# Three slots instead of two for the dilated attention, with its first jobs inside the gate block

## The reference

```
s = einsum(q, k) * DIL_SCALE           # per block: 128 queries, at most 2 x 128 keys
s = where(band & has_prev, s, -inf)
m = s.max(-1);  e = exp(s - m);  l = e.sum(-1);  acc = einsum(e, v)
...                                    # for each of the three groups, then
w = exp(m - m.max(groups));  o_b = sum(w * acc) / sum(w * l)
y_b = (o_b * silu(gb)) @ w_pb
```

## Time and profile before

| | |
|---|---|
| time, median of 3 runs | 1364.68 us (1364.15 to 1368.87) |
| profiled execution, its own time | 1366.24 us |
| its span | 1364.4 us, 22980 instructions |
| PE busy | 1218.7 us (89%) |
| DVE busy | 698.7 us (51%) |
| ACT busy | 509.3 us (37%) |
| POOL busy | 255.6 us (19%) |
| mean granted TensorE clock | 0.919 |

### The profile page before, as it was taken

One profiled execution on the slowest core, in us unless ns is written; L12 is line 12 of the kernel. 1 busy time (PEld: TensorE's weight loads), 2 busy tenths in 40 slices (PEclk: granted clock), 3 DMA queues, 4 the chain that ended last, 5 costly groups with the idle time before them and its releaser, 6 DMA issues.

```text
span 1364.4 us, 22980 instructions
## 1 busy us (share of the span) xinstructions
PE 1218.7 (89%) x7616; PEld 998.0 (73%) x7616; DVE 698.7 (51%) x1611; ACT 509.3 (37%) x1187; POOL 255.6 (19%) x262
## 2 busy tenths in 40 slices
PE   5897869998898799999977999998999899997987
PEld 1276757887687577787756999998998899997431
DVE  4317977176573332120414676766676667676421
ACT  1323545143243333323313554544454445453010
POOL 0033530266874003344420000000000000000000
PEclk9998869899998559999998999999999999998578
DMA  8632010122233003332264301323132323225005
GB/s 273 186 112 70 17 41 1 28 78 74 81 90 101 8 16 94 93 85 78 88 205 140 97 14 36 88 66 88 55 85 66 85 58 84 69 72 186 0 29 158
DMA packets 79418, 112.40 MB, mean 82 GB/s; under 512 B 8628, under 2 KB 50757, under 8 KB 79294
## 3 DMA queue, kind: packets, MB, share of 16 engines
q1 hardware_dynamic: 76214, 101.59, 26.0%
q0 software_dynamic: 1440, 5.11, 1.0%
q10 hardware_dynamic: 1648, 4.23, 0.9%
HBM read 105.21 MB, written 5.68 MB: 81 GB/s over the span
## 4 chain that ended last, share of the span: by engine, by line
PE 60%; DVE 15%; issue 8%; ACT 6%; POOL 5%; DMA 5%; SPq 2%; ACTq 0%; DVEq 0%; POOLq 0%
PE ps L1417 18%; PE ps L1081 6%; PE ps L1082 6%; PE ps L1083 6%; PE ps L1398 5%; PE ps L1096 3%; DVE ssq L2184 3%; PE ps L1443 3%; DMA raw<-in_w_ada 2%; ACT cT_hi L879 2%; PE ps L1463 2%; PE ps L1226 1%; PE ps L1220 1%; PE ps L1296 1%; PE ps L1307 1%
## 5 line engine op out<-in xcount | busy, mean ns | idle before, releaser
L960 POOL TENSOR_TENSOR wlo<-raw,whi 128x512 fp32r<-128x512 f32 (+3 forms) x148 | 171.3, 1161 | 447.1 <-ACT whi L624 446.9
L1081 PE MATMUL ps<-whi,hT_hi 128*128 128x512 f32 (+3 forms) x512 | 191.4, 374 | 31.0 <-POOL wlo L960 21.2
L1417 PE MATMUL ps<-wq_hi,cT_hi 128*128 128x260 f32 x1024 | 217.8, 294 | 0.4 <-ACT sq L908 0.4
L1417 PE MATMUL ps<-wq_hi,cT_lo 128*128 128x260 f32 x1024 | 206.8, 283 | 0.0
L1417 PE MATMUL ps<-wq_lo,cT_hi 128*128 128x260 f32 x1024 | 206.4, 283 | 0.0
L2184 DVE TENSOR_REDUCE ssq<-sq 128x8 f32<-128x512 f32 x256 | 172.6, 682 | 64.6 <-ACT sq L908 62.2
L624 ACT ACTIVATE whi<-raw 128x512 fp32r<-128x512 f32 (+3 forms) x148 | 83.2, 564 | 327.4 <-PE ps L1078 255.7
L1083 PE MATMUL ps<-whi,hT_lo 128*128 128x512 f32 (+3 forms) x512 | 187.1, 365 | 0.0
L1082 PE MATMUL ps<-wlo,hT_hi 128*128 128x512 f32 (+3 forms) x512 | 186.8, 365 | 0.0
L1417 PEld LDWEIGHTS ps<-wq_hi,cT_lo 128*128 128x128 f32 x1024 | 158.6, 189 | 0.0
L1417 PEld LDWEIGHTS ps<-wq_hi,cT_hi 128*128 128x128 f32 x1024 | 157.9, 190 | 0.8 <-ACT sq L908 0.8
(11 more groups left out here) (401 smaller groups left out, 1681.5 us busy)
## 6 DMA issues: line engine op xcount, KB each, us to landing
cn<-in_cache_mla SPq DMA_DIRECT2D x256, 144.0 KB, 2.1
raw<-in_w_in SPq DMA_DIRECT2D x64, 256.0 KB, 2.7
raw<-in_w_ada SPq DMA_DIRECT2D x48, 256.0 KB, 3.1
raw<-in_w_out SPq DMA_DIRECT2D x32, 256.0 KB, 3.0
sdk<-in_cw SPq DMA_DIRECT2D x3, 1536.0 KB, 11.2
raw<-in_w_in SPq DMA_DIRECT2D x32, 128.0 KB, 2.1
raw<-in_w_pa SPq DMA_DIRECT2D x16, 256.0 KB, 2.9
x_tiles<-in_x_prompt ACTq DMA_DIRECT2D x4, 512.0 KB, 5.6
```

Of the source, the lines that this page charges most:

```text
L960: nc.gpsimd.tensor_tensor(out=wlo[:, s % NHL, 0:width], in0=raw[:, j % NRAW, 0:width], in1=whi[:, s % NHL, 0:width].bitcast(F32), op=ALU.s ...
L1081: mm(out, hi[:, k, c], bh, start=st, stop=False)
L1417: last = mm(ps[:, 3 + 2 * (u % 2) + f, 0:260], a[c], wq[:, c, f, w], start=c == 0 and a is hi and wq is wq_hi, stop=c == 1 and a is lo)
```

## The change

Three things change, all around `pair_attention`.

**Banks.** The four tiles of `GB` take two banks, two tiles side by side in each (`PLACE`), with their sample rows in bank 7; the accumulation of a bank begins only with the tile at column 0 and is closed only by the second tile (`SHARES_BANK`). The items `TE` go to the banks of the tiles of `GA` as VectorE releases them (`HELD_BY`). The freed banks make three pairs of score banks. The turned bank and the output bank become single.

**Order around the gate.** `heads_turned(2)` moves from between `GA` and `GB` to ahead of chunk 2 of `GB`, and ScalarE rounds chunks 3 and 4 of `GB` ahead of its copies of those items. Ahead of chunk 4 both `qk(0)` and `qk(1)` are issued. ScalarE and VectorE do the exponentials and masks of jobs 0 and 1 before `GB` is copied out; each copy of a gate tile waits for both tiles of its bank.

**Order in the loop.** Masks, exponentials and scores are one job further ahead: TensorE `tr(n+1)`, `qk(n+3)`, `pv(n)`; VectorE copy of an even n, then `masks_max(n+2)`, `finish(n-1)`; ScalarE copy of an odd n, then `exp(n+2)`. `tr(n+1)` waits for the copy of n, and `pv(n)` for `finish(n-1)`. `pair_probs` becomes three tiles.

```diff
@@ -137,8 +137,23 @@
 MLA_JOBS = [(i, h, i + 1) for i in range(NT) for h in range(HM)]
-_gb = [(ITEM["GB"] + t) % BANKS for t in range(BANKS)]
-PAIR_SCORES, PAIR_OUT, PAIR_TURNED = ((_gb[5], _gb[6]), (_gb[0], _gb[1])), (_gb[3], _gb[4]), (7, _gb[2])
+_ga = [(ITEM["GA"] + t) % BANKS for t in range(BANKS)]
+PAIR_SLOTS, PAIR_AHEAD = 3, 2
+PAIR_SCORES, PAIR_OUT, PAIR_TURNED = (_ga[0:2], _ga[2:4], _ga[5:7]), 7, _ga[4]
+PLACE = {ITEM["GB"] + t: (_ga[5 + t // 2], t % 2 * BW) for t in range(NT)}
+PLACE[ITEM["GBs"]] = (7, 0)
+SHARES_BANK = [ITEM["GB"], ITEM["GB"] + 2]
+HELD_BY = {ITEM["GB"] + t: ITEM["GA"] - 2 + t // 2 for t in range(NT)}
+HELD_BY[ITEM["GBs"]] = None
+for _t in range(4):
+    PLACE[ITEM["TE"] + _t], HELD_BY[ITEM["TE"] + _t] = (_ga[_t], 0), ITEM["GA"] + _t
...
+
+def place(idx):
+
+    return PLACE.get(idx, (idx % BANKS, 0))
@@ -154,7 +169,7 @@
-    return 6 + chunk % 2 if chunk < N_MLA_CHUNKS else PAIR_TURNED[(chunk - N_MLA_CHUNKS) % 2]
+    return 6 + chunk % 2 if chunk < N_MLA_CHUNKS else PAIR_TURNED
@@ -328,7 +343,9 @@
         gb_sig = v3(put("gate_b_sigmoid", [P, NT * BW], V + 16 * K1), NT, BW)
-        pair_p = v3(put("pair_probs", [P, 2 * 512], W + 18432), 2, 512)
+        assert 229344 - V >= 62 * K1 + 256, 229344 - V
+        pair_p = [put(f"pair_probs{n}", [P, 512], o)[:, :]
+                  for n, o in enumerate((W + 18432, W + 20480, V + 60 * K1 + 256))]
@@ -629,7 +646,8 @@
             def bank(idx, w, n=P, start=0):
-                return ps[start:start + n, idx % BANKS, 0:w]
+                b, c = place(idx)
+                return ps[start:start + n, b, c:c + w]
@@ -705,23 +723,24 @@
                         h = 2 * hp + hh
-                        p = pair_p[:, n % 2, 256 * hh:256 * hh + nb * P]
+                        p = pair_p[n % PAIR_SLOTS][:, 256 * hh:256 * hh + nb * P]
...
-                split_to(FIRST["GB"] + COUNT["GB"])
-                exp(0)
+                for n in range(PAIR_AHEAD):
+                    exp(n)
...
                 for t in range(NT):
+                    act.wait_ge(z_done, ITEM["GB"] + t // 2 * 2 + 2)
...
                 for n in range(len(PAIR_JOBS)):
-                    if n + 1 < len(PAIR_JOBS):
-                        exp(n + 1)
...
                         pt_copy(act, nc.scalar.activation, N_MLA_CHUNKS + n, 2 * PAIR_JOBS[n][3], pt_a, (ACT.Copy,))
+                    if n + PAIR_AHEAD < len(PAIR_JOBS):
+                        exp(n + PAIR_AHEAD)
@@ -827,7 +846,9 @@
             mix_gates("GA", AW)
+            split_to(FIRST["GB"] + 5)
             heads_in_order(2, ITEM["TE"])
+            split_to(FIRST["GB"] + COUNT["GB"])
@@ -1047,8 +1068,9 @@
-                if idx >= BANKS:
-                    wait_evac(pe, idx - BANKS)
+                held = HELD_BY.get(idx, idx - BANKS if idx >= BANKS else None)
+                if held is not None:
+                    wait_evac(pe, held)
@@ -1071,8 +1093,9 @@
                             wait_bank(idx)
-                        out = ps[:, idx % BANKS, 0:w]
-                        st, en = k == 0, k == nk - 1
+                        bank, col = place(idx)
+                        out = ps[:, bank, col:col + w]
+                        st, en = k == 0 and col == 0, k == nk - 1
@@ -1080,7 +1103,7 @@
                             mm(out, hi[:, k, c], bl, start=False, stop=False)
-                            last = mm(out, lo[:, k, c], bh, start=False, stop=en)
+                            last = mm(out, lo[:, k, c], bh, start=False, stop=en and idx not in SHARES_BANK)
@@ -1100,7 +1123,7 @@
                 for col, rows_out_, src in parts:
-                    last = nc.tensor.transpose(ps[0:rows_out_, idx % BANKS, col:col + n_in], src, ident[0:n_in, 0:n_in])
+                    last = nc.tensor.transpose(ps[0:rows_out_, place(idx)[0], col:col + n_in], src, ident[0:n_in, 0:n_in])
@@ -1277,7 +1300,6 @@
             block_of("GA", ITEM["GA"], range(5), hThi, hTlo, hTs)
-            heads_turned(2, ITEM["TE"])
@@ -1285,9 +1307,10 @@
                     near, i, hp, nb = PAIR_JOBS[n]
-                    if n >= 2:
-                        pe.wait_ge(masked, N_MLA + n - 1)
-                    banks = PAIR_SCORES[n % 2]
+                    if n >= PAIR_SLOTS:
+                        pe.wait_ge(masked, N_MLA + n - PAIR_SLOTS + 1)
+                    slot = n % PAIR_SLOTS
+                    banks = PAIR_SCORES[slot]
@@ -1300,30 +1323,34 @@
                     pe.wait_ge(exp_done, N_MLA + n + 1)
-                    if n >= 2:
-                        wait_pt(pe, c - 2)
+                    if n >= 1:
+                        wait_pt(pe, c - 1)
...
                         o = 256 * (q // nb) + P * (q % nb)
-                        last = nc.tensor.transpose(ps[:, PAIR_TURNED[n % 2], q * P:(q + 1) * P], pair_p[:, n % 2, o:o + P], ident)
+                        last = nc.tensor.transpose(ps[:, PAIR_TURNED, q * P:(q + 1) * P], pair_p[n % PAIR_SLOTS][:, o:o + P],
+                                                   ident)
...
                 def first_scores(k):
-                    if k == 5:
+                    if k == 2:
+                        heads_turned(2, ITEM["TE"])
+                    elif k == 4:
...
                         qk(0)
+                        qk(1)
...
                 tr(0)
-                wait_evac(pe, ITEM["GB"] + 1)
-                qk(1)
+                wait_evac(pe, ITEM["GB"] + NT - 1)
+                qk(2)
...
                         tr(n + 1)
-                    if n + 2 <= last_job:
-                        qk(n + 2)
-                    if n >= 2:
-                        pe.wait_ge(o_done, N_MLA + n - 1)
+                    if n + PAIR_SLOTS <= last_job:
+                        qk(n + PAIR_SLOTS)
+                    if n >= 1:
+                        pe.wait_ge(o_done, N_MLA + n)
@@ -1335,7 +1362,7 @@
                                 vcl[:, b, i, h * 64:(h + 1) * 64]
-                            last = mm(ps[:, PAIR_OUT[n % 2], 64 * hh:64 * hh + 64], PT[:, c % 3, o:o + P], v_rows,
+                            last = mm(ps[:, PAIR_OUT, 64 * hh:64 * hh + 64], PT[:, c % 3, o:o + P], v_rows,
@@ -1965,13 +1992,14 @@
                     dve.wait_ge(qk_done, N_MLA + n + 1)
-                    if n >= 2:
-                        dve.wait_ge(trp_done, N_MLA_CHUNKS + n - 1)
-                    m = 4 * (n % 2)
+                    if n >= PAIR_SLOTS:
+                        dve.wait_ge(trp_done, N_MLA_CHUNKS + n - PAIR_SLOTS + 1)
+                    slot = n % PAIR_SLOTS
+                    m = 4 * slot
...
                     for hh in range(2):
-                        last = v.tensor_tensor_reduce(out=pair_p[:, n % 2, 256 * hh:256 * hh + w],
-                                                      in0=ps[:, PAIR_SCORES[n % 2][hh], 0:w], in1=msk, scale=1.0, scalar=NEG,
+                        last = v.tensor_tensor_reduce(out=pair_p[slot][:, 256 * hh:256 * hh + w],
+                                                      in0=ps[:, PAIR_SCORES[slot][hh], 0:w], in1=msk, scale=1.0, scalar=NEG,
@@ -1983,15 +2011,16 @@
                         else ocl[:, i, 2 * hp:2 * hp + 2, 0:DH]
-                    v.tensor_copy(out, ps[:, PAIR_OUT[n % 2], 0:2 * DH].rearrange("p (h e) -> p h e", h=2)).then_inc(o_done, 1)
-
-                masks_max(0)
+                    v.tensor_copy(out, ps[:, PAIR_OUT, 0:2 * DH].rearrange("p (h e) -> p h e", h=2)).then_inc(o_done, 1)
+
+                for n in range(PAIR_AHEAD):
+                    masks_max(n)
...
                 for n in range(len(PAIR_JOBS)):
-                    if n + 1 < len(PAIR_JOBS):
-                        masks_max(n + 1)
...
                         pt_copy(dve, v.tensor_copy, N_MLA_CHUNKS + n, 2 * PAIR_JOBS[n][3], pt_d, ())
+                    if n + PAIR_AHEAD < len(PAIR_JOBS):
+                        masks_max(n + PAIR_AHEAD)
```

## The result

| | before | after |
|---|---|---|
| median on the same chip | 1366.58 us (1364.15 to 1368.87, 4 runs) | 1324.04 us (1316.57 to 1327.92, 4 runs) |
| ratio | | 0.9692, 95% interval 0.9654 to 0.9729 |
| profiled execution: own time, span | 1366.24, 1364.4 us | 1321.37, 1319.6 us |
| mean granted TensorE clock | 0.919 | 0.945 |

The change made the kernel 3.1% faster.

A forecast was written before the change was run, and what follows sets the result against it. The prediction took the pair loop's wait on exponentials with two slots, 4.48 us a job at half clock, as the bound. Gains of 34.6 (loop), 1.9 (exit) and 2.4 (gate) sum to 38.9, giving 1326 us, range 1321 to 1356.

The forecast's parts named there:

- Clock, full (0.60): TensorE's clock stays full from the gate through the pair loop; loop gains 34.6 us, 1326 us in all; chance 0.60.
- case (a): Clock falls at the pair loop's entry and stays at half; gain 11.5 us, hence 1353 us; chance 0.27.
- Entry: Start of the pair loop: turning 1 at +2.3 us, turning 2 at +4.7; TensorE holes of 0.5, 0.9 and 1.2.
- Job at full clock: Pair loop: TensorE's turning, scores and values take 1.91 us per job at full clock; 2.0 was priced.
- the ring of 2.0: Pair loop: the single turned bank's chain of copies, masks and exponentials takes 4.0 us over two jobs, 2.0 per job.
- The three splits: Three odd jobs in the loop carry a weight split of 0.61 us ahead of the copy, 1.8 in all.
- Output bank: Pair loop: the single bank's wait for finish(n-1) is hidden by turning and scores; without that cover, 0.5 us a job.
- Loop: The pair jobs at full clock: 4.7 + 12 jobs x 2.0 + 1.8 + 4.4 = 34.9 us, gain 34.6.
- Gate: Gate block before the pair loop ends at 441.5 us, gain 2.4, with the clock half until 432.08.
- (b): Slower: single banks cost 0.5 us a job in the loop, and the clock returns later in the gate; 1368; chance 0.04.
- (d): Masks and copies hide nothing new because TensorE is the bound; loop gives nothing, gate 2.4 us; 1362; chance 0.02.
- case (e): Clock falls at the loop's entry and comes back in the packed loop, losing 6 us; 1332; chance 0.04.

The follow-up runs named there:

- spread_turns: Changed kernel with the four items of turned heads spread, one ahead of each of gate chunks 2 to 5, first scores ahead of chunk 6; 1348.62 us.
- spread_entry: spread_turns with VectorE's first copy ahead of the gate's sample rows, TensorE waiting for these only ahead of the first values; 1345.31 us.
- vector_copies: Changed kernel with all sixteen copies out of the turned bank on VectorE, none on ScalarE; 1324.43 us, one profiled execution at 1345.41.
- all_three: spread_turns and vector_copies together, with VectorE taking the sample rows behind its second copy and TensorE waiting for them only ahead of the first values; 1317.41 us.
- hole_at_entry: Changed kernel with 70 linked small VectorE memsets ahead of its take of the gate's sample rows, making TensorE idle at the loop's entry; 1350.01 us.
- scores_late: Changed kernel with the scores of jobs 0 and 1 issued behind the gate block instead of ahead of its chunk 4; 1353.0 us.
- copies_behind: Changed kernel with masks and exponentials of job n+2 ahead of the copy of job n, on VectorE and ScalarE; 1359.51 us.
- two_slots: Changed kernel with two slots of probabilities instead of three, and one job ahead instead of two; 1363.6 us.
- before_filled: Kernel before the change with throwaway 128x512 matmuls ahead of each turning in the pair loop; 1353.05 us.
- spread_filled: spread_turns with eight throwaway matmuls, four ahead of turning 1 and four ahead of the values of job 0; 1322.63 us.

## Why the prediction was right, step by step

*Time.* 1326.0 predicted, 1324.04 measured. Of the sum itself, 38.9 predicted, the edited stretches show 37.5; what made the total larger lies outside of them, so that the total came out within 2 us is in part luck.

*Clock, full (0.60).* Right in its outcome, and in part by luck: 1.00 from 428 to the end of the loop, but the reason given was weak. I argued that no new hole is as long as the 2.49 us through which the clock had stayed. spread_turns and spread_entry lost the clock with holes of 0.93, 0.79 and 1.42, all shorter, and in spread_turns with the very holes of the kernel after. The length of a single hole does not decide. The kernel after differs from spread_turns ahead of the entry: its own turning inside the gate block had brought the clock down (0.75 over 425 to 430) and it came back about 9 us before the entry. That alone doesn't protect the entry: the profiled vector_copies has the same fall (0.79 over 425 to 430, back to 1.00 over 435 to 440) and lost its clock at the entry with holes of 0.29, 0.93 and 0.29. Nor is it needed: all_three kept 1.00 from 410 on, over holes of 0.29 and 0.62. Why the entry of the kernel after kept its clock in nine of nine executions stays open; what the runs show is that entries with 1.5 to 2.0 us of holes in all came out either way. A 0.27 for case (a) was not too much: hole_at_entry, scores_late, spread_turns and spread_entry all land there, and vector_copies once.

*Case (a)* was priced at 3.98 a job, 60.4 for the loop and 1353. hole_at_entry shows 3.91, 60.9 (440.84 to 501.74), 2.1 of it the longer hole, and 1350.

*Entry.* Turning 1 at +2.3 and turning 2 at +4.7, predicted; +2.30 and +4.72, measured. Holes 0.5, 0.9, 1.2 predicted; 0.29, 0.93, 0.79 measured.

*Job at full clock.* This term was too small. TensorE's issue was put at 0.44 + 0.63 + 0.84 = 1.91, from the MLA attention, and the ring of 2.0 was to be the bound. Measured: 0.54 + 0.63 or 0.65 + 0.94, together 2.11 for near and 2.13 for far jobs, so TensorE sets it; from turning 3 on, a turning waits for a copy out of the turned bank only at the splits. The missing 0.2 is 0.10 behind the turning and 0.10 behind the values. PEld is TensorE's weight load; two of its rows from the kernel before, MLA attention, then two from the kernel after:

```profile
225.12 0.30 PEld L1226 LDWEIGHTS ps<-kTm,qTm 96*128 96x128 f32 x2
...
225.67 0.19 PEld L1220 LDWEIGHTS ps<-v_mla,PT 128*128 128x128 f32 x1 [0.24 <-issue]
```

```profile
450.69 0.52 PEld L1319 LDWEIGHTS ps<-dkT,dqT 64*128 64x128 f32 x8 [0.17 <-issue]
451.34 0.97 PEld L1365 LDWEIGHTS ps<-kvo,PT 128*128 128x128 f32 x8
```

In the MLA attention the first weights of the scores and of the values are loaded 0.11 and 0.42 ahead of their first matmuls (225.23 and 226.09). In the pair loop both loads start only with their first matmuls (450.69 and 451.34), and the one ahead of the scores waits 0.17 for nothing shown. Taking the issue times of one stage for the other left this out; why the loads come later here no run shows.

Twelve jobs with their splits took 26.5 (441.87 to 468.37), 25.8 predicted. The three splits themselves were over-priced: their steps were 2.43, 2.56 and 2.55 against 2.13, together 1.15 for 1.8.

*Output bank.* In the loop its wait is hidden, as predicted; at the end the cover is gone, and the last values and the merge block each wait 0.39 for `finish`. The last two jobs took 5.0 for 4.4. Loop 34.9 predicted, 36.2 measured.

*Gate.* Gain 2.4 predicted, 2.3 measured, for partly another reason. I had the clock half through the holes and until 432.08; it stayed at 1.00 to about 424, into the last of the three holes, and was full again at 428. All of this block lies 4.4 us earlier than the prediction's times, so its end is 437.15 and not 441.5.

*Rivals.* (b): the single banks never cost 0.5 a job with the copies ahead; copies_behind shows that they do with the copies behind. (d): two_slots shows that the third slot is not idle. The Trainium skill, "TensorE: Matmul & The Clock Gate", "Why this matters for your kernels", names as the remedy for half clock to keep TensorE busy without a break. The runs with filled holes, before_filled and spread_filled, agree as long as the clock is up. Once it is down, 54 us of closed work in hole_at_entry did not raise it, and by that rule hole_at_entry would have come out near the 1332 of case (e) instead of 1350.

## What to carry to other kernels

Read the granted clock beside each stage of TensorE, and price a change there at both levels: the third slot was worth 0.57 us a job at half clock and 1.37 at full. Prices taken from another stage can leave out how that stage overlaps its weight loads: here 1.91 us a job was predicted and 2.13 measured. Where a stage of small matmuls begins after a dense one, close its first few microseconds before anything else, with later work or with matmuls thrown away. And look at every execution, not at the median alone: there one program can go either way.

## What the runs showed of the hardware

A VectorE operation of 128x2 waited for GpSimd. In the kernel after, `tensor_scalar` (L2006) takes 0.17 to 0.20 us each time but three; these three start inside a GpSimd operation of 1.27 us and end with it (454.39 + 1.07 and 454.16 + 1.27). Timeline of the kernel after, VectorE and GpSimd:

```profile
452.27 0.17 DVE L2006 TENSOR_SCALAR o_by_class<-amax 128x2 f32<-128x2 f32 x1
454.39 1.07 DVE L2006 TENSOR_SCALAR o_by_class<-amax 128x2 f32<-128x2 f32 x1
458.96 1.19 DVE L2006 TENSOR_SCALAR o_by_class<-amax 128x2 f32<-128x2 f32 x1
463.66 1.18 DVE L2006 TENSOR_SCALAR o_by_class<-amax 128x2 f32<-128x2 f32 x1
```

```profile
454.16 1.27 POOL L981 TENSOR_TENSOR wlo<-raw,whi 128x512 fp32r<-128x512 f32 x1 [20.54 <-ACT whi L641]
458.86 1.27 POOL L981 TENSOR_TENSOR wlo<-raw,whi 128x512 fp32r<-128x512 f32 x1 [3.43 <-ACT whi L641]
463.55 1.27 POOL L981 TENSOR_TENSOR wlo<-raw,whi 128x512 fp32r<-128x512 f32 x1 [3.43 <-ACT whi L641]
```

The Trainium skill, "SBUF — State Buffer", "SBUF: two separate sides", describes an exclusive lock on a port pair that VectorE and GpSimd share: a GpSimd operation on one side, and on the other a VectorE operation in a mode that uses two ports, or with two inputs in SBUF; whoever comes second waits until the other has ended. The trace agrees in the waiting; in which mode this operation ran no run shows. Having masks two jobs ahead hides most of the delay here: the turnings right behind the first two, at 456.85 and 461.55, came 2.14 after the ones before them. The turnings after those, at 459.41 and 464.10, came 2.56 and 2.55 later; these are steps with a split, and the first such step (to 454.71), ahead of any of the three delays, took 2.43. The 0.13 between them fits the delay, which VectorE passes on without a pause (exponentials of job 10 begin 0.32 behind a turning, those of job 8 0.19), but no run takes it away.
